# DeltaNet stage: the output gate's projection moved from the inverse into the chain, the loop over heads written out, the convolution of v split over two levels

## The chip, the core and the metric

One core of one Trainium2 chip runs the whole program. The metric is device microseconds of one execution, median of the runs. TensorE does the matmuls, VectorE (DVE in the rows), ScalarE (ACT) and GpSimd (POOL) the element-wise work, SyncE (SP) issues the DMAs here. A matmul takes a stationary operand, which is loaded first (LDWEIGHTS, PEld in the rows), and a moving one, and writes PSUM, which has 8 banks of 512 float32 a partition. Every float32 matmul of the program stands as two instructions in the trace.

## What is computed

One layer of a diffusion backbone on 128 context and 512 latent tokens of width 1024. Its token mixer has two branches, a bidirectional gated DeltaNet and a state-space one; the change is in the DeltaNet branch alone. Of each of its 8 heads (width 128; h here is the input of the mixer):

```python
qkv = silu(dwconv_centred(h @ w_qkv, conv_w, conv_b))     # 5 taps over time
q, k = l2norm(q) * DK ** -0.5, l2norm(k)
beta, g = sigmoid(beta_raw), -exp(a_log) * softplus(a_raw + dt_bias)
# for each direction, chunk by chunk: T = (I + strict(beta k k^T * decay))^-1
v_new = T @ (v * beta) - T @ (k * beta * exp(gc)) @ S
o = (q * exp(gc)) @ S + (q k^T * decay) @ v_new
S = S * exp(g_last) + kdec^T @ v_new
# the sum of both directions
o = rms(o_fwd + o_bwd) * norm_w * silu(h @ w_z)            # the output gate
```

`h @ w_z` is the projection that the change moves. The final states S of both directions are outputs too.

## The kernel before

`build` runs stages one after the other; `deltanet` is one of them, between 690 and 1531 us of the profiled execution. Each engine has its program, written as a Python function, and the engines are ordered by semaphores alone: what stands where in an engine's queue is laid out by hand.

The 640 tokens are 5 tiles of 128 (tile 0 is the context). Each head h goes through `inverse(h)` and `chain(h)`. Constants n = h + 1, K, Q, V, Z = 0 to 3.

**Projections.** `proj(n, j, i)` (L665) is a fifth of projection j of head n: i = 0 to 3 are two of the 8 blocks of the inner dimension each, over the 512 latent tokens (L672), i = 4 all 8 blocks over the 128 context tokens (L675). Latent results go to bank 5 (K, V) or 6 (Q, Z), context results to bank 7. ScalarE copies K, Q, V out (`raw`, L909, L910), VectorE convolves them over time (`convolve`: one tensor-scalar at L1124, then four scalar-tensor-tensor taps at L1126, each waiting for the one before), ScalarE takes tanh (`tanh`, L916), VectorE makes the silu of it (`silu`, L1135, L1136). The squares of k and q (L920) are summed over columns by TensorE (`sums`, L695), kept by VectorE (`keep_sums`, L1141), and GpSimd takes the inverse root (`roots`, L1054). TensorE turns k (`turn_k`), VectorE scales it to kn (`keep_kn`, L1153), TensorE turns kn back (`turn_kn`), ScalarE keeps it (`keep_knT`, L929, L930). v is turned by `turn_v` and kept in `vt` by `keep_v` (L934, L935). The turns are L681.

**Inverse.** The triangular inverse of 10 blocks (5 tiles, two directions) in three groups is built in 6 levels: TensorE multiplies (`blocks_DT`, L743), turns (`turn_D`, L752) and multiplies (`blocks_X`, L735); ScalarE copies the results out (L954, L959) and VectorE masks X (`mask_X`, L1185, and for the last group L1190 adds the identity). At five places i of each level l, `between` puts other work in TensorE's queue: the rest of K's projection of the next head in level 0, Q's in level 1, V's in level 2, **the gate's projection of the current head in level 3** (for head 0 it stands in the prologue), the sums in level 4, the turns of kn and v in level 5. VectorE and ScalarE do the matching steps between their own: `convolve` in levels 1 to 3, `silu` in 2 to 4, `keep_sums`, `gate` and `keep_kn` in level 4. The gate is tanh on ScalarE (`tanh_z`, L924, L925, into `zth`, which shares the memory of R, vn, vd, qs) and `gate` on VectorE (L1145, L1146, into `zg`); `gated` (L1208, L1209) multiplies the turned output of the previous head by it in level 0. Before the levels stand the first two fifths of K's projection, then L809 and turns that start the inverse.

**Chain.** Five steps p; step 0 is the context tile, steps 1 to 4 take one tile forward and one backward. In each TensorE multiplies the state by k and q (KS L848, QS L851; not in step 0), VectorE forms R (L1247 in step 0, else L1249), TensorE VNEW = T R (L855), ScalarE scales it twice (vd L1012, vn L1017), TensorE makes the state's update SU from vd (L867; not in step 4), VectorE the state (L1257, L1259), TensorE the output product O from vn (L875), VectorE adds it to `osum` (L1273, L1276), GpSimd adds the scaled QS (L1078, L1080). Between them stands work for the next head: the k-k and k-q products (L719), the decay sums (`segments`, L726, L727), ScalarE's exponentials (`decay`, L941, L943) and copies (L949), VectorE's masks (`strict`, L1160; `keep_M`, L1168; L1174, L1179 in step 4). GpSimd builds the masks of the next head (L1060, L1064) when level 5 has its last X.

**Loops and loads.** Heads 0 and 7 are written out; heads 1 to 6 are a loop of the engine itself with two heads in its body (`Fori(1, GH - 2, 2)`, three rounds) on TensorE, ScalarE, GpSimd and VectorE, and a loop over one head on SyncE, for heads 1 to 5. SyncE's `body(h)` waits for the last QS of the head before and loads a state, waits for head h+1's three projections and loads K, Q, V weights of head h+2, waits for the gate's projection (`g_z`) and loads the next gate weights, then stores the context's final states. Before the loop the prologue of TensorE is: all four projections of head 0, sums, turns, products, segments.

The order in the prologue and the chain's heart before:

```python
for j in range(4):                       # prologue, L886
    for i in range(5): ...; proj(0, j, i)
sums(0, 0); turn_kn(0, 0); turn_v(0, 0)
for b in range(3): products(0, 0, b)
segments(0)
inverse(0, 0, first=True); chain(0, 0)
```

## Time and profile before

| | us |
|---|---|
| median of 3 runs | 2403.32 (2402.17 to 2407.29) |
| the profiled execution | 2399.45 |
| its span, first to last instruction | 2397.6 |
| TensorE busy in the span | 2137.0 (89%) |
| VectorE busy | 999.7 (42%) |
| ScalarE busy | 540.0 (23%) |
| GpSimd busy | 274.5 (11%) |
| mean granted TensorE clock, 1 is 2.4 GHz | 0.950 |

In the rows below a line of a view in order of time has the start in us from the span's start, the length in us, the engine, the line of the kernel, the operation, output and inputs, shapes and how many instructions were merged, and in brackets the time for which the engine stood idle before it and what ended that: an engine with the line of its instruction, or "issue", when nothing in the profile released it. Lengths of matmuls overlap with the start of the next: what an instruction takes of TensorE's time is read from start to start. In the view by windows the columns are the window, its length, and for PE, PEld, DVE, ACT and POOL the busy us with the number of instructions, then the granted clock, the DMA share and GB/s. In the view by line: the group, its count, busy us and mean ns, and idle us before it.

### The profile page before, as it was taken

To read this page: it belongs to the slowest core of one execution; us is meant where nothing else is said; L and a number is where in the kernel's file an instruction comes from. 1 tells how busy PE (TensorE), PEld (TensorE's weight loads), DVE (VectorE), ACT (ScalarE), POOL (GpSimd) and SP (SyncE) were. 2 spreads that over 40 slices of the span, in tenths; PEclk is the share of its full clock that TensorE was granted. 3 is DMA by queue.
4 is the path that set the end of the run, shared out by engine and by line. 5 is a ranking of instruction groups with operands and counts; after the bars stand their busy time and mean duration, and the time that the engine had idled before them with its cause. 6 is when DMAs were issued, how large, how long until landed. Compare 5 with 4: busy or idle time off the path is not lost. (4 is left out here: it accounts for less than half of the span.)

```text
span 2397.6 us, 26673 instructions
## 1 busy us (share of the span) xinstructions
PE 2137.0 (89%) x10098; PEld 1329.9 (55%) x10098; DVE 999.7 (42%) x1920; ACT 540.0 (23%) x1283; POOL 274.5 (11%) x325
## 2 busy tenths in 40 slices
PE   3899999999978998989989898799999795799985
PEld 1555555555545777767767777455555444443332
DVE  3446556555544555544545544200000066322224
ACT  1323213233112433333333334200000000011111
POOL 0020020201110102111110211100000000321112
PEclk9899999999988999999999999999999896799998
DMA  8121201211020100101011001495322365499983
GB/s 292 51 62 44 53 10 44 62 44 36 9 66 12 38 25 18 36 6 38 4 40 30 11 11 30 145 297 174 110 79 80 125 247 202 139 396 413 398 324 136
DMA packets 177806, 260.06 MB, mean 108 GB/s; under 512 B 14759, under 2 KB 146664, under 8 KB 163344
## 3 DMA queue, kind: packets, MB, share of 16 engines
q1 hardware_dynamic: 151096, 219.04, 26.6%
q10 hardware_dynamic: 18488, 23.54, 3.4%
q0 software_dynamic: 8096, 15.75, 1.8%
q8 instruction: 84, 1.38, 0.2%
q14 instruction: 42, 0.34, 0.0%
HBM read 231.78 MB, written 39.10 MB: 113 GB/s over the span
## 5 line engine op out<-in xcount | busy, mean ns | idle before, releaser
L672 PE MATMUL bank<-hT,shared 128*128 128x512 f32 x512 | 244.9, 608 | 14.0 <-DMA shared<-in_w_in_dram 7.9
L1421 PE MATMUL bank<-hT,shared 128*128 128x512 f32 x384 | 169.3, 594 | 2.6 <-DVE xT L1794 1.8
L2393 PE MATMUL bank<-ring,xgT 128*64 128x512 f32 (+1 forms) x416 | 150.1, 627 | 13.7 <-DMA ring<-in_w_exp_up_dram 9.9
L1185 DVE TENSOR_TENSOR X<-bank,negm 128x512 f32<-128x512 f32 x144 | 81.8, 599 | 185.7 <-PE bank L735 185.5
L1476 PE MATMUL bank<-wz,hT 128*128 128x512 f32 x320 | 152.5, 614 | 0.0
L672 PEld LDWEIGHTS bank<-hT,shared 128*128 128x128 f32 x512 | 91.5, 196 | 89.2 <-issue 81.1
L743 PE MATMUL bank<-DT,X 128*128 128x128 f32 x960 | 128.8, 277 | 2.4 <-DVE X L1185 2.4
L743 PEld LDWEIGHTS bank<-DT,X 128*128 128x128 f32 x960 | 119.9, 192 | 17.0 <-issue 13.4
L735 PE MATMUL bank<-D_,MT 128*128 128x128 f32 x960 | 125.2, 280 | 0.0
L1975 DVE SCALAR_TENSOR_TENSOR prod<-gth,bank 128x512 f32<-128x512 f32 x16 | 11.0, 687 | 272.1 <-PE bank L1945 272.1
L954 ACT COPY D_<-bank 128x512 f32<-128x512 f32 x144 | 73.3, 515 | 215.8 <-PE bank L752 215.6
L1421 PEld LDWEIGHTS bank<-hT,shared 128*128 128x128 f32 x384 | 71.1, 190 | 84.3 <-issue 84.1
L735 PEld LDWEIGHTS bank<-D_,MT 128*128 128x128 f32 x960 | 117.2, 196 | 0.4
L1945 PE MATMUL bank<-yT,wm 128*128 128x512 f32 x256 | 111.2, 592 | 0.0
L2393 PEld LDWEIGHTS bank<-ring,xgT 128*64 128x64 f32 (+1 forms) x416 | 56.5, 165 | 96.5 <-issue 96.5
L1945 PE MATMUL bank<-hT,wm 128*128 128x512 f32 x224 | 98.0, 595 | 0.0
L959 ACT COPY DT<-bank 128x512 f32<-128x512 f32 x144 | 74.0, 518 | 95.5 <-PE bank L743 94.4
L1476 PEld LDWEIGHTS bank<-wz,hT 128*128 128x128 f32 x320 | 59.5, 196 | 63.2 <-issue 63.2
L1465 PEld LDWEIGHTS bank<-xT,M 128*128 128x128 f32 x640 | 78.6, 197 | 19.3 <-DVE xT L1776 11.1
L752 PEld LDWEIGHTS bank<-cst,DT 128*128 128x128 f32 x480 | 61.3, 146 | 46.6 <-issue 46.3
L1744 DVE SCALAR_TENSOR_TENSOR sroom<-spadded,scw,sroom 128x644 f32<-128x644 f32 x96 | 85.4, 890 | 3.4
L1126 DVE SCALAR_TENSOR_TENSOR conv<-padded,cw,conv 128x644 f32<-128x644 f32 x96 | 85.4, 890 | 3.4
(405 smaller groups left out, 3394.6 us busy)
## 6 DMA issues: line engine op xcount, KB each, us to landing
shared<-in_w_in_dram SPq DMA_DIRECT2D x62, 512.0 KB, 5.5
ring<-in_w_exp_gate_dram SPq DMA_DIRECT2D x26, 1024.0 KB, 12.9
ring<-in_w_exp_up_dram SPq DMA_DIRECT2D x26, 1024.0 KB, 17.6
ring<-in_w_exp_down_dram SPq DMA_DIRECT2D x26, 1024.0 KB, 14.6
aw<-in_w_ada_dram SPq DMA_DIRECT2D x8, 2048.0 KB, 9.6
yd<-mzero ACTq DMA_DIRECT2D x1, 16128.0 KB, 107.2
aw<-in_w_ada_dram SPq DMA_DIRECT2D x8, 1024.0 KB, 21.1
wz<-in_w_in_dram SPq DMA_DIRECT2D x4, 2048.0 KB, 7.9
```

The source lines that it names most:

```text
L672: pe.matmul(bank[LATB[j]][:, :], wof(j)[:, k, :], hT[:, k, SEQ:T], start=(k == 0), stop=(k == KD - 1), skip_group_check=True)
L735: last = pe.matmul(xdv(g)[:, u * P:(u + 1) * P], MT[:, u0 + u, :], D_[:, u0 + u, :], start=True, stop=True, skip_group_check=True)
L743: last = pe.matmul(dtv(g)[:, u * P:(u + 1) * P], X[:, u0 + u, :], DT[:, u0 + u, :], start=(g == 2), stop=(g == 2 or l == LEVELS - 1), skip ...
L959: act.copy(DT[:, u0:u0 + m, :], tiles4(dtv(g))).then_inc(s["g_DTkept"], 1)
L1126: ins = STT(out=to, in0=x[:, k:k + CW], scalar=cw[:, k, j:j + 1], in1=to, op0=ALU.mult, op1=ALU.add)
L1185: ins = TT(out=X[:, u0:u0 + m, :], in0=tiles4(xdv(g)), in1=mask, op=ALU.mult)
L1421: pe.matmul(bank[a][:, :], wn(n)[:, k, :], hT[:, k, SEQ:T], start=(k == 0), stop=(k == KD - 1))
L1465: last = pe.matmul(bank[Y][:, h * SP_:(h + 1) * SP_], M[:, u % 2, h, :], dtx[:, d, h * SP_:(h + 1) * SP_], start=(d == 0 and h == 0), stop ...
L1476: last = pe.matmul(bank[Z][:, :], hT[:, k, t * P:(t + 1) * P], wz[:, k, :], start=(k == 0), stop=(k == KD - 1), skip_group_check=True)
L1744: ins = STT(out=c3, in0=padded[:, n % 3, k:k + CW], scalar=cw[:, k, n:n + 1], in1=c3, op0=ALU.mult, op1=ALU.add)
L1945: last = pe.matmul(bank[j][:, :], W(at + k), src[:, k, SEQ:T], start=(k == 0), stop=(k == kk - 1))
L2393: last = pe.matmul(bank[2 + slot][at, :], xgT[:, slot, k, at], wgu[w][:, k, :, :], start=(k == 0), stop=(k == KD - 1))
```

## The change

The gate's projection of head h leaves level 3 (and the prologue) for `chain(h)`: its latent part is written in eight chunks of one block each (`gate_lat`), one after QS and one after VNEW in steps 1 to 4, into bank 0; its context part (`gate_ctx`) in chunks of two blocks after O in steps 1 to 3 and one after VNEW in step 4, into bank 2. `tanh_z` and `gate` stand at the end of the chain on ScalarE and VectorE, `zth` is a part of `th`, and the next inverse waits for the gate before it writes banks 0 and 2. The loops over heads are Python loops, on all engines. v's projection starts one place later (latent part in level 2, context part in level 3); its first two taps are in level 3, its last three in level 4, its tanh and silu in step 0 of the chain; its turn and copy stand in levels 1 and 2 of its own head's inverse, with one buffer in place of two. In the prologue the segments, the decay and the strict masks come ahead of the sums.

```diff
-        vt = S("vt", [P, 2, NT, P])
+        vt = S("vt", [P, NT, P])
-        zth = small4[:, :, :, :].rearrange("p a d n -> p (a d n)")[:, 0:T]
+        zth = th[:, 0:T]
-        LATB = (5, 6, 5, 6)
+        LATB = (5, 6, 5, 0)
+        CTXB = (7, 7, 7, 2)
@@ sync
-                with sp.Fori(1, GH - 2) as h:
+                for h in range(1, GH - 2):
                     body(h)
@@ tensor
+                def gate_lat(h, k):
+                    pe.matmul(bank[LATB[Z]][:, :], wof(Z)[:, k, :], hT[:, k, SEQ:T], start=(k == 0), stop=(k == KD - 1), skip_group_check=True)
+
+                def gate_ctx(h, ks):
+                    for k in ks:
+                        last = pe.matmul(bank[CTXB[Z]][:, 0:P], wof(Z)[:, k, :], hT[:, k, 0:SEQ], start=(k == 0), stop=(k == KD - 1), skip_group_check=True)
+                    return last
-                def turn_v(n, h):
-                    pe.wait_ge(s["g_zg"], h + 1)
-                    pe.wait_ge(s["g_silu"], 3 * n + 3)
-                    pe.wait_ge(s["g_knT"], n + 1)
-                    turned(vT, 6, P, s["g_vturn"])
+                def turn_v(h, more):
+                    if more:
+                        pe.wait_ge(s["g_raw"], 3 * h + 4)
+                    pe.wait_ge(s["g_silu"], 3 * h + 3)
+                    turned(vT, 5, P, s["g_vturn"])
@@ between
-                    if l == 2 and more:
-                        if i == 0 or i == 4:
-                            pe.wait_ge(s["g_raw"], 3 * n + 1 + i // 4)
-                        proj(n, V, i)
-                    if l == 3:
-                        if more and i == 4:
-                            turn_k(n)
-                        if not first:
...
-                            proj(h, Z, i)
+                        if i == 4:
+                            turn_v(h, more)
+                    if l == 2 and more and i > 0:
+                        if i == 1:
+                            pe.wait_ge(s["g_v"], h + 1)
+                        proj(n, V, i - 1)
+                    if l == 3 and more and i == 0:
+                        pe.wait_ge(s["g_raw"], 3 * n + 2)
+                        proj(n, V, 4)
+                    if l == 3 and more and i == 4:
+                        turn_k(n)
-                    if l == 5 and more and i == 2:
-                        turn_v(n, h)
@@ inverse, before the first product
+                    if not first:
+                        pe.wait_ge(s["g_zg"], h)
@@ chain, step p, after QS
+                            if p == 1:
+                                pe.wait_ge(gw[Z], 16 * h + 16)
+                                if more:
+                                    pe.wait_ge(s["g_dec"], n + 1)
+                                else:
+                                    pe.wait_ge(s["g_DTkept"], 18 * h + 18)
+                            gate_lat(h, 2 * p - 2)
@@ after VNEW
+                        if p > 0:
+                            gate_lat(h, 2 * p - 1)
+                        if p == 4:
+                            gate_ctx(h, range(6, 8)).then_inc(s["g_z"], 1)
@@ after O
+                        if 1 <= p <= 3:
+                            gate_ctx(h, range(2 * p - 2, 2 * p))
@@ prologue
-                for j in range(4):
+                for j in (K, Q, V):
...
-                sums(0, 0)
+                pe.wait_ge(s["g_gm"], 1)
+                segments(0)
+                turn_k(0)
+                sums(0)
                 turn_kn(0, 0)
-                turn_v(0, 0)
                 for b in range(3):
                     products(0, 0, b)
-                segments(0)
                 inverse(0, 0, first=True)
                 chain(0, 0)
-                with pe.Fori(1, GH - 2, 2) as h:
-                    for a in range(2):
-                        inverse(h + a, 1 - a)
-                        chain(h + a, 1 - a)
+                for h in range(1, GH - 1):
+                    inverse(h, h % 2)
+                    chain(h, h % 2)
@@ scalar, inverse
+                        if l == 2:
+                            keep_v(h)
-                        if more and 1 <= l <= 3:
+                        if more and 1 <= l <= 2:
                             raw(n, l - 1)
-                        if l == 4 and not first:
-                            tanh_z(h)
-                        if more and 2 <= l <= 4:
-                            tanh(n, l - 2)
+                        if more and 2 <= l <= 3:
+                            tanh(n, l - 2, wait=(l == 3 or not first))
                         keep_DT(h, l, 0)
+                        if more and l == 3:
+                            raw(n, V)
@@ scalar, chain, end of step 0 and end of the chain
                             decay(h + 1)
+                            tanh(h + 1, V)
...
+                    tanh_z(h)
@@ vector, inverse
-                        if more and 2 <= l <= 4:
+                        if more and 2 <= l <= 3:
                             silu(n, 1 - par, l - 2)
-                        if more and 1 <= l <= 3:
+                        if more and 1 <= l <= 2:
                             convolve(n, l - 1)
-                        if l == 4:
-                            if more:
-                                keep_sums(n)
-                            if not first:
-                                gate(h)
-                            if more:
-                                keep_kn(n, 1 - par)
+                        if more and l == 3:
+                            convolve(n, V, taps=range(2))
+                        if more and l == 4:
+                            keep_sums(n)
+                            convolve(n, V, taps=range(2, TAPS))
+                            keep_kn(n, 1 - par)
@@ vector, chain, after the output sum of step 0 and at the end
+                        if more and p == 0:
+                            silu(n, 1 - par, V)
...
+                    gate(h)
```

The loops of ScalarE, GpSimd and VectorE are written out in the same way as TensorE's.

## Rows read from the trace of the kernel before

**Rows 1.** Busy time by head: microseconds, busy per engine (count), granted clock, DMA share, GB/s.
```profile
848.02:947.24 99.22, 92.27 (x580) 71.48 (x579) 52.85 (x115) 36.25 (x95) 14.10 (x20) 1.00 0.10 25
947.24:1051.84 104.60, 94.60 (x579) 72.34 (x578) 52.87 (x115) 36.25 (x95) 14.11 (x20) 0.97 0.09 24
```

**Rows 2.** TensorE in order of time, last head's levels 2 to 4: start, length, instructions.
```profile
1474.56 1.95 PE L743 MATMUL bank<-DT,X 128*128 128x128 f32 x16
...
1480.22 1.06 PE L743 MATMUL bank<-DT,X 128*128 128x128 f32 x8
...
1492.65 1.95 PE L675 MATMUL bank<-hT,shared 128*128 128x128 f32 x16
1494.44 1.95 PE L743 MATMUL bank<-DT,X 128*128 128x128 f32 x16
```

**Rows 3.** TensorE in order of time, start of head 4's inverse, level 5 and chain.
```profile
1148.45 3.60 PE L672 MATMUL bank<-hT,shared 128*128 128x512 f32 x8
1151.89 1.02 PE L809 MATMUL bank<-DT,cst 128*128 128x512 f32 x2
...
1219.85 1.16 PE L743 MATMUL bank<-DT,X 128*128 128x128 f32 x8 [0.42 <-DVE X L1185]
...
1231.90 0.71 PE L855 MATMUL bank<-small,DT 128*128 128x128 f32 x4 [0.26 <-DVE small L1249]
...
1237.12 0.71 PE L855 MATMUL bank<-small,DT 128*128 128x128 f32 x4 [1.23 <-DVE small L1249]
...
1240.51 0.61 PE L851 MATMUL bank<-state,kq 128*128 128x128 f32 x4
1241.41 0.71 PE L855 MATMUL bank<-small,DT 128*128 128x128 f32 x4 [0.29 <-DVE small L1249]
1242.84 0.71 PE L867 MATMUL bank<-small,shared 128*128 128x128 f32 x4 [0.71 <-ACT small L1012]
...
1244.25 0.71 PE L848 MATMUL bank<-state,kq 128*128 128x128 f32 x4 [0.18 <-DVE state L1259]
...
1247.12 0.71 PE L875 MATMUL bank<-small,att 128*128 128x128 f32 x4 [0.71 <-ACT small L1017]
```

**Rows 4.** All engines in order of time, from head 2's last step to head 3.
```profile
1041.04 0.71 PE L855 MATMUL bank<-small,DT 128*128 128x128 f32 x4 [0.29 <-DVE small L1249]
...
1044.50 0.47 DVE L1276 TENSOR_TENSOR gboth<-gboth,bank 128x128 f32<-128x128 f32 x2
...
1046.23 5.78 PE L672 MATMUL bank<-hT,shared 128*128 128x512 f32 x8 [3.05 <-issue]
```

**Rows 5.** VectorE in order of time, prologue.
```profile
724.30 0.69 DVE L1136 SCALAR_TENSOR_TENSOR kq<-th,conv 128x512 f32<-128x512 f32 x1
```

**Rows 6.** Groups of instructions of the DeltaNet stage by line.
```profile
L1126 DVE SCALAR_TENSOR_TENSOR conv<-padded,cw,conv 128x644 f32<-128x644 f32 x72 | 64.1, 890 | 2.5
...
L916 ACT ACTIVATE th<-conv 128x644 f32<-128x644 f32 x18 | 13.5, 750 | 0.0
...
L1160 DVE TENSOR_TENSOR D_<-dec,D_ 128x640 f32<-128x640 f32 x12 | 9.8, 819 | 0.0
```

**Rows 7.** ScalarE in order of time, first step of head 4's chain.
```profile
1229.70 1.08 ACT L943 ACTIVATE dec<-bank 128x512 f32<-128x512 f32 x2
```

**Rows 8.** TensorE in order of time, prologue.
```profile
729.72 2.39 PE L695 MATMUL bank<-cst,gboth 128*128 128x1 f32 x20 [1.48 <-ACT gboth L920]
...
745.53 3.60 PE L672 MATMUL bank<-hT,shared 128*128 128x512 f32 x8
753.07 1.64 PE L809 MATMUL bank<-DT,cst 128*128 128x512 f32 x2 [3.94 <-DVE DT L1179]
```

**Rows 9.** VectorE in order of time, head 4, level 4.
```profile
1215.58 0.17 DVE L1141 TENSOR_SCALAR ssum<-bank 128x10 f32<-128x10 f32 x1 [1.59 <-PE bank L695]
```

**Rows 10.** GpSimd in order of time, head 4, level 4.
```profile
1215.83 1.95 POOL L1054 TENSOR_TENSOR rn<-ssum,half 128x10 f32<-128x10 f32 x1 [54.42 <-DVE ssum L1141]
```

**Rows 11.** Line 1190 (X plus identity): shortest, median, longest in ns.
```profile
L1190 DVE TENSOR_TENSOR X<-X,cst x48: 424/426/1508, 760.7 to 1500.9; 128x256 f32<-128x256 f32 x48
```

More of the change, by code:

```diff
@@ L1039, in _ @@
                 chain(0, 0)
-                with act.Fori(1, GH - 2, 2) as h:
-                    for a in range(2):
-                        inverse(h + a, 1 - a)
-                        chain(h + a, 1 - a)
+                for h in range(1, GH - 1):
+                    inverse(h, h % 2)
+                    chain(h, h % 2)
                 inverse(GH - 1, 1, more=False)
@@ L1096, in _ @@
                 chain(0, 0)
-                with pool.Fori(1, GH - 2, 2) as h:
-                    for a in range(2):
-                        chain(h + a, 1 - a)
+                for h in range(1, GH - 1):
+                    chain(h, h % 2)
                 chain(GH - 1, 1, more=False)
```

104 lines of the change are left out of this document (44 added, 60 removed).

## The prediction

> **What bounds the kernel now.** I read the busy time by head first. In the DeltaNet stage TensorE is busy in 92.27 of the 99.22 us of an ordinary head [rows 1], and VectorE, ScalarE and GpSimd in half of it or less. So a head lasts as long as TensorE's program: six levels of the inverse, then the chain of five steps. The second view is TensorE's own order in time. In the last head, where the inverse has nothing beside it but the gate projection, a bare level runs from 1474.56 to 1480.22, 5.66 us, with no wait. The level that holds the gate projection runs to 1494.44, 14.22 us [rows 2]. So the inverse has no idle time for the projection to fill: it costs 14.22 - 5.66 = 8.56 us a head. Third, the chain [rows 3], where TensorE waits in every step: 0.3 us (once 1.23) for VectorE's R, 0.7 for ScalarE's scaled copies, 0.2 for the state. That idle time is what the change fills. Fourth, heads 2 and 4, at whose ends the loop returns to its top, last 104.60 us instead of 99.22 [rows 1]; the surplus shows as 3.05 us marked "issue" and eight matmuls in 5.6 us instead of 3.44, right behind the last product of the chain [rows 3, 4].
>
> **The sum**, against the profiled execution: 2399.45 us, 3.87 under the median of 2403.32; its span is 2397.6.
>
> 1. Gate projection out of level 3, heads 1 to 7: 7 x 8.56 = **-59.9**. V's context part (the same form, 8 matmuls of 128 columns, 1.79 us by 1492.65 to 1494.44 [rows 2]) only goes from level 2 to level 3, and the turn of v from level 5 to level 1: nothing. The cover of a level without filler is shown by the last head: 5.66 with no wait. With q's silu, ScalarE's copy of V and two taps beside it, TensorE's 8 us for level 3 still exceed the DVE's some 5.4.
>
> 2. The loops written out. The return to the loop's top happens twice (after heads 2 and 4): 2 x (104.60 - 99.22) = **-10.8**. About 3.1 of the 5.4 is TensorE waiting for nothing but its next instruction, the rest the eight matmuls after it, partly at 1.2 instead of 2.4 GHz (granted clock 0.97 over the head against 1.00 [rows 1]). The Trainium skill's Runtime: NRT & Kernel Launch, section Instruction fetch mechanics, says that a taken branch out of the fetched window stalls while code in a straight line streams unseen; the boundary row agrees, the sum stands without it. Bounds: 0 and 10.8.
>
> 3. Prologue, where today head 0's gate projection runs before anything of the chain: q's silu ends at 724.99 on VectorE [rows 5], and a square of 0.74 (as ScalarE's tanh, 0.750 [rows 6]) follows, so the column sums could start at 725.9; they start at 729.72 since ScalarE sits in the gate's tanh first: -3.8. From products to inverse, the segment products, ScalarE's decay (0.4 + 1.08 [rows 7]) and two strict masks of 0.82 [rows 6] move ahead of the sums, 2.0 + 1.5 + 1.6, into idle time: -5.1 of the 7.5 us between 745.53 and 753.07 and the 2 before it [rows 8]. Together **-9**, bounds -4 (only the sums come earlier) and -12 (the low clock there goes too).
>
> 4. The chain pays. One pass of a gate chunk over 512 columns is 3.44 / 4 = 0.86 us (1148.45 to 1151.89 [rows 3]), two context chunks 0.45.
> - Chunk between QS and the product after it (step 3): QS starts at 1240.51, the product at 1241.41, 0.90; QS fills 0.45 of it. A chunk makes 1.31: +0.41. In step 2 the product waits 1.23 for VectorE anyway: 0.
> - Chunk after that product: next product 1.43 later (1241.41 to 1242.84), 0.45 + 0.86 = 1.31 fits: 0.
> - Two context chunks after the output product: 1242.84 to 1244.25 is 1.41 and holds two groups of products of 0.54 and 0.45; with 0.45 more it is 1.44: +0.03.
> - Last step: a chunk and two context chunks, 0.45 + 0.86 + 0.45 = 1.76 against 1.43 (0.71 idle at 1247.12 [rows 3]): +0.33.
> - Step 1 has V's silu (0.29 + 0.68 with overlap, 0.9) ahead of R on VectorE. ScalarE's decay ends at 1230.78 [rows 7]; tanh 0.75 behind it, silu 0.9, R 0.6: R would be ready at 1233.1, and the product that takes it starts at 1231.90 today [rows 3]: +1.2, and 0.1 for the wait's end: +1.3. (The turn of v no longer stands ahead, which takes 0.55 from both alike and is paid in level 1.)
> Sum for heads 0 to 6: 1.3 + 0 + 0.44 + 0.44 + 0.33 = 2.5, **+17.5**. Last head, no silu and no masks: 4 x 0.44 + 0.33 = **+2.1**. Bounds a head: 1.2 (silu hidden) and 5 (each chunk exposed by half more).
>
> 5. Level 4: VectorE now has three taps between the sums it keeps and the writes of kn. A tap is 0.89 with 0.03 between [rows 6]. Sums are kept at 1215.58 + 0.17 [rows 9], GpSimd's root ends at 1215.83 + 1.95 = 1217.78 [rows 10]; three taps end at 1218.5. kn, and behind it the mask X that level 5 waits for already (0.42 at 1219.85 [rows 3]), come 0.7 later. 7 x 0.7 = **+4.9**, bounds 0 and 1.5 a head. Split in two the taps otherwise cost nothing: all five in the short level 3 would pass its mask by 2.
>
> 6. Handover. Bank 0 and bank 2 hold the gate, so the next inverse waits for VectorE's gate(h), which is queued behind first blocks, add one and the last output sum: that sum ends at 1044.97, 3.9 us after the last product that R feeds (1041.04 [rows 4]); it starts 0.4 earlier against that product now, and the gate adds 0.28 + 0.68, the size of a silu: 4.5. TensorE arrives after 1.76 + 0.45 + 3.44 = 5.65, K's first half covering it: 0. Before head 7 there is no K: 4.5 against 2.2, **+2.3** once.
>
> 7. DMAs. SP's load of the next gate weights, the state store and, behind them, the next state's load are queued behind the gate's end in the chain rather than in level 3; the weights are wanted a whole inverse (some 60 us) later: 0. Q, K, V loads wait one level longer, also with tens of us in hand. GpSimd gets no work. ScalarE's tanh of the gate stands before the next keep D, both after TensorE's K half: 0.
>
> Total -59.9 - 10.8 - 9 + 17.5 + 2.1 + 4.9 + 2.3 = **-52.9**: 2346.5 in a profiled execution of that kind, and 3.87 more, **2350**, as median.
>
> **Rivals.**
> - *Boundary stays.* The 5.4 us belong to code fetch that long straight code pays too. For it: the code grows threefold. Against it: heads 0, 1 and 7 stand in or enter straight code without it. +10.8: 2361. Chance 0.08.
> - *VectorE and GpSimd block each other in level 4.* The taps read two tensors in SBUF while GpSimd takes its root. The row for X plus identity shows such a pairing: 424 ns alone, 1508 beside GpSimd's masks [rows 11]. If the taps wait for the whole root, 1.95 a head: +13.7, 2364. Against it: most of the 1.95 on 10 columns is not reading, and if GpSimd waits for a tap instead, its result is wanted only after the third. Chance 0.06. The Trainium skill's SBUF — State Buffer, section Who interferes with whom, states this as a rule against the change: a VectorE instruction with two SBUF inputs and a GpSimd one that reads SBUF exclude each other for a whole instruction. By it the sum would be 2364; no row here shows a tap beside a root.
> - *The gate isn't covered* (the other side). If products of the chain are issued no earlier than now after each chunk, all 8.67 us of a projection land in the chain, 7.5 more a head than counted: 8 x 7.5 = +60, 2410. It takes 52.9 / 8 = 6.6 us a head to turn the sign. Against it: the 0.7 us waits are on ScalarE, which doesn't wait for gate chunks, and banks 0 and 2 are free. Chance 0.03; half of it, 0.02, gives 2380.
> - *More comes back*: silu finds VectorE idle, the prologue gives 12, no wait in level 5: -3 - 9 - 4.9 against the sum, partly: 2338. Chance 0.11.
>
> **The numbers.** The forecast has 0.70: 2350, own range 2340 to 2360. The range 2338 to 2366 takes in the first two rivals and most of the last; outside it stays under 0.2. About 0.2% (5 us) is what a measurement can tell from no change: faster 0.95, same 0.02, slower 0.03.
>
> **What will show it.** Level 3 near 8 us for heads 1 to 6, 5.7 for head 7, with no L672 matmuls in it but V's. Chain steps: 4.7 us where they were 4.3, 5.2 kept in step 2, about 7 from the first to the second. No 3 us "issue" gap in the stage. A wait near 1.1 for X at level 5. Inverse of head 0 starting near 744. Heads of some 93 to 94 us. Wrong if the 0.7 us waits for vd stay beside the chunks, if level 3 shows waits of over 0.5, or if straight code shows gaps marked "issue".

## The result and the profile after

The changed kernel takes **2336.72 us** (median of 4 runs, 2334.37 to 2337.98), the kernel before 2402.74 in the 4 runs beside it: ratio 0.9727, 95% interval 0.9715 to 0.974, 66 us less. The forecast was 2350.0 with a range of 2338 to 2366: the direction and the mechanism held, the time lies 1.3 us below the range. Profiled execution against profiled execution it is 2399.45 to 2336.3, -63.15, where the sum said -52.9. The other 2.9 us are the distance of profile and median: 3.3 in the runs of before beside it, 0.4 in those of after.

The head of the page after, then, in a second fence, busy time by head with the columns of [rows 1]:

```profile
span 2334.2 us, 25709 instructions
...
PE 2110.1 (90%) x10098; PEld 1314.7 (56%) x10098; DVE 995.9 (43%) x1920; ACT 540.4 (23%) x1283; POOL 276.2 (12%) x325
```

```profile
835.70:928.86 93.16, 90.30 (x580) 70.38 (x579) 52.08 (x115) 36.27 (x95) 14.68 (x20) 1.00 0.10 26
928.86:1022.00 93.14, 90.28 (x579) 70.39 (x578) 51.65 (x115) 36.28 (x95) 16.38 (x20) 1.00 0.10 26
```

These are heads 1 and 2. A head has as many TensorE instructions as before and lasts 93.2 us instead of 99.22 or 104.60 [rows 1], with 2.9 us of it idle instead of 6.95. Next, TensorE in order of time for head 4's levels 3 to 5, its chain and the start of head 5, the stretch that answers to [rows 3]:

```profile
1159.05 1.05 PE L751 MATMUL bank<-DT,X 128*128 128x128 f32 x8
1159.94 1.95 PE L676 MATMUL bank<-hT,shared 128*128 128x128 f32 x16
...
1167.06 1.95 PE L751 MATMUL bank<-DT,X 128*128 128x128 f32 x16
...
1176.02 1.16 PE L751 MATMUL bank<-DT,X 128*128 128x128 f32 x8 [1.00 <-DVE X L1201]
...
1181.78 0.61 PE L866 MATMUL bank<-small,DT 128*128 128x128 f32 x4
...
1188.51 0.71 PE L866 MATMUL bank<-small,DT 128*128 128x128 f32 x4 [0.48 <-DVE small L1264]
1189.05 1.02 PE L680 MATMUL bank<-hT,shared 128*128 128x512 f32 x2
1189.93 0.71 PE L882 MATMUL bank<-small,shared 128*128 128x128 f32 x4
...
1193.73 0.71 PE L866 MATMUL bank<-small,DT 128*128 128x128 f32 x4 [0.37 <-DVE small L1264]
...
1198.42 0.61 PE L866 MATMUL bank<-small,DT 128*128 128x128 f32 x4
...
1203.01 0.61 PE L866 MATMUL bank<-small,DT 128*128 128x128 f32 x4
...
1205.21 3.60 PE L673 MATMUL bank<-hT,shared 128*128 128x512 f32 x8
1208.64 1.02 PE L814 MATMUL bank<-DT,cst 128*128 128x512 f32 x2
```

Level 3 lasts 1167.06 - 1159.05 = 8.01 us and holds no projection but V's context part (L676). In the chain a gate chunk (L680) stands where the wait of 0.7 us for ScalarE was, and the product behind it (L882) waits for nothing. From product to product (L866) the four steps take 6.73 (1181.78 to 1188.51), 5.22, 4.69 and 4.59. Before, they were 5.72 (from the first line below to the L855 at 1231.90 in [rows 3]), 5.22, 4.28 and 4.28:

```profile
1226.18 0.61 PE L855 MATMUL bank<-small,DT 128*128 128x128 f32 x4
...
1245.69 0.71 PE L855 MATMUL bank<-small,DT 128*128 128x128 f32 x4 [0.28 <-DVE small L1249]
```

The output products go straight over into K's projection, with no "issue" gap [rows 4].

The prologue, on TensorE in order of time [rows 8]:

```profile
723.10 4.24 PE L703 MATMUL bank<-cst,gboth 128*128 128x1 f32 x20 [4.06 <-ACT gboth L935]
731.59 1.33 PE L690 MATMUL bank<-cst,shared 128*128 128x128 f32 x5 [4.26 <-DVE shared L1169]
733.76 4.00 PE L727 MATMUL bank<-kq 128*128 128x256 f32 x10 [0.84 <-ACT kq L946]
...
742.62 1.10 PE L814 MATMUL bank<-DT,cst 128*128 128x512 f32 x2 [1.43 <-DVE DT L1195]
```

From the stage's first projection to the first product of the inverse it takes 54.97 us instead of 62.83. The sums start 4.0 us earlier against that first projection, but take 4.24 instead of 2.39 at a low clock. The wait ahead of the inverse is 1.43 instead of 3.94.

**Where the time went, head by head.** Each row is the distance from one head's first product of the inverse (L809 before, L814 after) to the next head's; head 7 counts to the first instruction of its last product T R.

| | before | after | measured | forecast |
|---|---|---|---|---|
| prologue | 62.83 | 54.97 | -7.9 | -9 |
| head 0 | 94.95 | 93.06 | -1.9 | +3.2 |
| head 1 | 99.21 | 93.16 | -6.1 | -5.4 |
| head 2 (returned) | 104.60 | 93.16 | -11.4 | -10.8 |
| head 3 | 100.05 | 93.48 | -6.6 | -5.4 |
| head 4 (returned) | 104.68 | 93.16 | -11.5 | -10.8 |
| head 5 | 101.10 | 93.16 | -7.9 | -5.4 |
| head 6 | 96.97 | 92.27 | -4.7 | -3.1 |
| head 7 | 65.14 | 60.27 | -4.9 | -6.5 |
| sum | | | -62.9 | -53 |

### The profile page after: what moved, and what is told of

Same layout as the page of the kernel before. It is cut to its first block and busy times, and to the rows that moved or that the text cites. A ratio compares the mean times of both kernels' runs of the same rounds, so it can differ in the third digit from the quotient of the medians.

```text
span 2334.2 us, 25709 instructions
## 1 busy us (share of the span) xinstructions
PE 2110.1 (90%) x10098; PEld 1314.7 (56%) x10098; DVE 995.9 (43%) x1920; ACT 540.4 (23%) x1283; POOL 276.2 (12%) x325
## 5 line engine op out<-in xcount | busy, mean ns | idle before, releaser
L673 PE MATMUL bank<-hT,shared 128*128 128x512 f32 x384 | 180.6, 600 | 8.0 <-DMA shared<-in_w_in_dram 8.0
L1433 PE MATMUL bank<-hT,shared 128*128 128x512 f32 x384 | 169.3, 594 | 2.6 <-DVE xT L1806 1.8
L1433 PEld LDWEIGHTS bank<-hT,shared 128*128 128x128 f32 x384 | 71.1, 190 | 84.3 <-issue 84.1
L673 PEld LDWEIGHTS bank<-hT,shared 128*128 128x128 f32 x384 | 67.9, 193 | 63.3 <-issue 55.1
L2141 PE MATMUL bank<-ring,shared 128*128 128x512 f32 x160 | 72.9, 617 | 15.4 <-DMA ring<-in_w_o_dram 15.4
```

Of the source, the lines that this page charges most:

```text
L673: pe.matmul(bank[LATB[j]][:, :], wof(j)[:, k, :], hT[:, k, SEQ:T], start=(k == 0), stop=(k == KD - 1), skip_group_check=True)
L1433: pe.matmul(bank[a][:, :], wn(n)[:, k, :], hT[:, k, SEQ:T], start=(k == 0), stop=(k == KD - 1))
```

## The experiments

The table leaves 10 us to explain. The theory for them: the terms of the sum are right in kind, but it priced every head as head 1, and left standing what heads 0, 3, 5 and 6 had beside it. Rivals: the written-out loops bring more than the 5.4 us a return (other engines' loops too), or the gate costs the chain less than counted.

**1. The loops written out alone.** Kernel before, with all loops over heads written out:

```diff
-                with pe.Fori(1, GH - 2, 2) as h:
-                    for a in range(2):
-                        inverse(h + a, 1 - a)
-                        chain(h + a, 1 - a)
+                for h in range(1, GH - 1):
+                    inverse(h, h % 2)
+                    chain(h, h % 2)
```

> The kernel before with the loops over heads written out on every engine and nothing else. Theory (the two returns of the loop cost 5.4 us each): 10.8 us less than before, ratio 0.9955, heads 2 and 4 at 99.2 us, no gap marked issue. Rival (code fetch is paid in straight code too): within 3 us of before, with new gaps marked issue in heads 1 to 6. Rival on the clock (the return to the top also brings the low clock of other heads): 14 to 17 us less, and the stretches at 1.2 GHz in heads 3, 5 and 6 gone.

2392.57 us, ratio 0.9946 (0.993 to 0.9963). The DeltaNet stage is 10.5 us shorter, against 10.8 of the sum. The end of head 2 on TensorE:

```profile
1049.72 0.71 PE L875 MATMUL bank<-small,att 128*128 128x128 f32 x4 [0.72 <-ACT small L1016]
1050.26 3.60 PE L672 MATMUL bank<-hT,shared 128*128 128x512 f32 x8
1053.70 1.02 PE L809 MATMUL bank<-DT,cst 128*128 128x512 f32 x2
```

No gap, and 3.44 us for the eight matmuls. But heads 1 to 6 are not all 99.2: they take 100.13, 100.04, 100.91, 99.14, 99.14 and 96.46 (head 6 without K's half). So head 4 is at the 99.2 that was expected, but head 2 is not: some surplus has moved from heads 5 and 6 to heads 1, 2 and 3, which experiment 3 takes up.

**2. The loops put back, one group at a time**, into the changed kernel: TensorE's, and then those of all the others.

```diff
@@ tensor; in the second kernel scalar, gpsimd, vector and sync instead
-                for h in range(1, GH - 1):
-                    inverse(h, h % 2)
-                    chain(h, h % 2)
+                with pe.Fori(1, GH - 2, 2) as h:
+                    for a in range(2):
+                        inverse(h + a, 1 - a)
+                        chain(h + a, 1 - a)
```

> The changed kernel with TensorE's loop over heads restored, those of the other engines written out. Theory (TensorE's own return is what costs): 10 to 11 us more than the changed kernel, ratio near 0.977, heads 2 and 4 about 5.4 us longer, a gap of 3 us marked issue at each. Rival (the gap is another engine's return, seen from TensorE): the time of the changed kernel, ratio 0.973.

> The changed kernel with the loops of ScalarE, VectorE, GpSimd and SyncE restored, TensorE's written out. Theory: the returns of these engines now stand behind the gate's tanh and product at the end of the chain, whose result TensorE waits for with 1.1 us in hand; a return of 2 to 3 us (VectorE's first work after its return in the kernel before is not needed for 5 us) makes heads 2 and 4 up to 2 us longer: 0 to 4 us more than the changed kernel, ratio 0.973 to 0.975. Rival: all engines' returns cost alike, 10 us more, ratio 0.977.

TensorE's loop: 2347.5, ratio 0.9766 (0.9745 to 0.9787). The others': 2339.93, 0.9733 (0.9717 to 0.9749), DeltaNet stage 767.09 us to the last of the four instructions of its last product T R, where the changed kernel has 767.03. The two returns of TensorE, in order of time:

```profile
1024.74 0.61 PE L890 MATMUL bank<-small,att 128*128 128x128 f32 x4
1028.11 3.70 PE L673 MATMUL bank<-hT,shared 128*128 128x512 f32 x8 [2.77 <-issue]
1031.64 1.02 PE L814 MATMUL bank<-DT,cst 128*128 128x512 f32 x2
...
1217.93 5.39 PE L673 MATMUL bank<-hT,shared 128*128 128x512 f32 x8 [2.84 <-issue]
1223.16 1.02 PE L814 MATMUL bank<-DT,cst 128*128 128x512 f32 x2
```

The return of TensorE's queue lengthens head 2 by 3.0 us, and head 4 by 4.8, where the matmuls behind it run at the low clock (5.39 us for eight): 7.8 together, under the 10 to 11 that were expected. The whole time of the two kernels, run side by side, is 7.6 us apart. Returns of the other four queues cost nothing that the stage shows. The Trainium skill's Runtime: NRT & Kernel Launch, section Instruction fetch mechanics, has a taken branch out of the fetched window stall and straight code stream on unseen. The traces agree: 2.8 us idle at each return of TensorE, and no such gap behind heads 2 and 4 where its program is written out. The prediction's rival that the boundary's cost stays in straight code is out.

**3. The kernel before once more**, with no edit.

> The kernel before, unchanged, for a second trace. If the stretches at 1.2 GHz in heads 0, 3, 5 and 6 follow from what the program does, they stand at the same places and the head lengths are the same within 0.3 us (94.95, 99.21, 104.60, 100.05, 104.68, 101.10, 96.97). If they fall by chance, the two heads with the returns keep theirs and the others move by 1 to 2 us. Ratio 1.000.

2404.37 us, heads 0 to 6 94.94, 99.21, 104.67, 100.0, 104.65, 101.09 and 97.48. Six of them agree within 0.1 us, head 6 is 0.5 longer: at its end three VectorE instructions (L1174) take 1.88 us beside 1.46 for two of GpSimd (L1080), where the first execution has 1.62 beside 3.15. Here are windows of 3.4 us, with the columns of [rows 1], of the kernel before in the first execution:

```profile
1320.10:1323.50 3.40, 3.40 (x18) 3.40 (x18) 1.96 (x7) 1.54 (x3) 1.95 (x1) 0.50 0.00 0
1323.50:1326.90 3.40, 3.40 (x33) 3.40 (x32) 2.65 (x6) 0.65 (x3) 1.12 (x1) 1.00 0.02 5
```

in the second (its stage starts 1.5 us later):

```profile
1321.60:1325.00 3.40, 3.40 (x18) 3.40 (x18) 2.02 (x8) 1.55 (x3) 1.96 (x1) 0.51 0.00 0
```

and of the kernel with the loops written out alone, where this stretch is gone and others, like one in head 2's inverse, have come:

```profile
1018.40:1021.80 3.40, 3.40 (x18) 3.37 (x17) 1.98 (x6) 1.26 (x4) 1.15 (x1) 0.51 0.00 0
...
1320.10:1323.50 3.40, 2.98 (x27) 2.79 (x26) 3.37 (x8) 0.85 (x2) 2.12 (x2) 1.00 0.00 0
```

The heads' surplus over 99.2 are single stretches of 3.4 us in which the granted clock is 0.50, 1.2 GHz, and TensorE does some half of its matmuls (18, against 33 in the window behind). In heads 0 to 6 they are no accident of one execution: both executions have the same seven there, apart from the returns. In head 7 they can be: the second execution has one 12 us into its inverse, behind the wait of 2.8 us for the turned output, and the first has none; that inverse takes 49.78 us with it and 48.14 without, 1.6 more. They are no property of a head either, since with another length of the heads the seven stand in others. But from head 0's level 1 to head 6 they have only two places, in this kernel and in all the others of this study (a loop's return aside): right behind the sums of level 4, twenty matmuls of one column (some 10 to 12 us ahead of the chain's first product), and in the chain, behind steps with waits (12 to 14 us after that product, 8 to 9 in experiment 5). The kernel before has one at its start in head 0 (after the wait of 3.94 us), behind the sums in heads 0, 5 and 6, and in the chain in heads 0, 3 and 5. The changed kernel:

```profile
1078.30:1081.70 3.40, 3.40 (x18) 3.40 (x17) 3.33 (x8) 1.42 (x3) 2.17 (x1) 0.50 0.00 0
1358.20:1361.60 3.40, 3.40 (x18) 3.40 (x18) 3.33 (x8) 1.37 (x4) 2.07 (x1) 0.50 0.00 0
1406.00:1409.40 3.40, 3.40 (x19) 3.40 (x18) 1.34 (x3) 0.96 (x2) 0.00 (x0) 0.50 0.00 0
```

The wait ahead of the third of them, on TensorE in order of time:

```profile
1404.84 0.77 PE L690 MATMUL bank<-cst,gboth 128*128 128x128 f32 x5 [2.80 <-DVE gboth L1219]
```

The changed kernel has them behind the sums (heads 0, 3 and 6), where they cost 0.3 us instead of 0.9 to 1.1, since level 5 waits 1.00 us behind them anyway, and one in head 7 behind a wait of 2.8 us. This one costs 1.6 us: the inverse of head 7 takes 41.77 us with it, and 40.13 and 40.14 in the kernel of experiment 8 and the second of experiment 4, which have none there. **In the chain the changed kernel has none.** That holds for all ten profiles of kernels of this study with every chunk in the chain (a loop's return aside), in 70 chains ahead of a next head. The kernels with the old waits in the chain have three in seven (the kernel before, both executions, and with its loops out) or six in seven (experiment 5); with one chunk of eight kept there is one, with four kept none (experiment 4). So some 7.4 us of such stretches, of which some 2.7 stood in the chain, became 2.6. With the chunks in the waits, no chain has a stretch; experiment 5, which differs from the changed kernel in the place of the gate's work alone, has them in six chains. But that the empty waits alone bring them is not shown: experiment 4 with one chunk has nearly the waits of the kernel before in steps 2 to 4, and one stretch where that has three. Why one head has a stretch and its neighbour none stays open.

**4. What the gate's chunks cost in the chain.** Only the first of the eight latent chunks kept; then those after QS left out (outputs lack the missing part of the gate):

```diff
@@ gate_lat
-                    pe.matmul(bank[LATB[Z]][:, :], ...)
+                    if k == 0:
+                        pe.matmul(bank[LATB[Z]][:, :], ...)
```

> The changed kernel with one of the eight chunks of the gate's latent projection left in the chain and seven left out, so the output lacks seven eighths of that projection. It asks what the chunks cost where they are now. Theory (they fill waits): step 3 and 4 from 4.69 and 4.59 back to 4.3, the first two steps unchanged at 6.7 and 5.2, 1.0 to 1.3 us a head and 1.6 in the last, 9 to 10 us in all if the clock stays. Clock theory (the chunks in the waits are what keeps the chain at 2.4 GHz): the stretches at 1.2 GHz come back in the chain of three or four heads at 0.8 to 1 us each, so that only 5 to 7 us are left, ratio 0.970 to 0.971. Rival (chunks are exposed in full): 7 x 0.86 us a head, 48 us, ratio 0.953.

> The changed kernel without the chunks between QS and VNEW (half of the gate's latent projection left out), those behind VNEW kept. Theory: those were exposed only in steps 3 and 4 (and 1 to 4 of the last head), 0.4 and 0.3 us: 0.7 x 7 + 1.4 = 6 us less than the changed kernel, ratio 0.970; steps 6.7, 5.2, 4.3, 4.3, and no wait longer than today's behind VNEW. Rival (the chunk behind VNEW delays the next product too): the same 6 us and steps that stay above 4.5.

One chunk: 2334.97, ratio 0.9705 (0.9681 to 0.973). Heads take 92.22 instead of 93.16. The theory that the chunks keep the clock up expected stretches in three or four chains; there is one, in head 0. TensorE in order of time, steps 1 to 3 of head 4's chain:

```profile
1189.12 0.71 PE L867 MATMUL bank<-small,DT 128*128 128x128 f32 x4 [0.48 <-DVE small L1265]
1190.55 0.71 PE L883 MATMUL bank<-small,shared 128*128 128x128 f32 x4 [0.72 <-ACT small L1029]
...
1194.35 0.71 PE L867 MATMUL bank<-small,DT 128*128 128x128 f32 x4 [1.22 <-DVE small L1265]
...
1198.63 0.71 PE L867 MATMUL bank<-small,DT 128*128 128x128 f32 x4 [0.28 <-DVE small L1265]
```

Without the chunks the waits of [rows 3] are back (0.72, 1.22, 0.28), and the last two steps are 4.28 again. So seven chunks of 0.86 us, 6.0 us of TensorE's time, cost 0.94 us a head, which the sum had at 0.41 + 0.41 + 0.33 = 1.15. The stage is 4.5 us shorter than in the changed kernel, less than these 0.94 a head, as head 0 has the stretch in its chain and head 7 one more at its start. In the whole time neither this kernel nor the next can be told from the changed one. Without the four after QS alone: 2333.74, 0.971 (0.9687 to 0.9732); steps 3 and 4 are 4.28 again, the end of the chain (from its last product T R to the next head's first) 5.74, where it is 5.41 with one chunk, and heads 92.60. So the chunk after QS is what steps 3 and 4 pay, and the chunk in the last step adds the 0.33 of the sum.

**5. The gate back in level 3**, of all eight heads (head 0's too, which no longer has it in the prologue), its tanh and product in level 4, everything else as changed:

```diff
-        LATB = (5, 6, 5, 0)
-        CTXB = (7, 7, 7, 2)
+        LATB = (5, 6, 5, 6)
+        CTXB = (7, 7, 7, 7)
@@ between, level 3
+                        if i < 4:
+                            gate_lat(h, 2 * i)
+                            gate_lat(h, 2 * i + 1)
+                        else:
+                            gate_ctx(h, range(8)).then_inc(s["g_z"], 1)
```

> The changed kernel with the gate's projection back in level 3 (of every head), its tanh and product in level 4, all else as changed. Theory: 8 x 8.56 in the inverse, less the 0.94 a head that the chain pays for it, 1.6 in the last head and 2.2 at head 7's start, plus 0.9 a head since the gate's product stands ahead of the taps in level 4: 63 to 66 us more than the changed kernel, level with the kernel before, ratio 0.998 to 1.000. Rival (a bare level 3 hides less, so the projection filled real waits there): 50 us or less, ratio under 0.994, with waits in the changed kernel's level 3 that vanish here.

2406.44 us, ratio 1.0013 (1.0002 to 1.0023): all of the gain is gone, though the loops are written out. TensorE, head 3, level 5 and the chain:

```profile
1119.58 1.16 PE L751 MATMUL bank<-DT,X 128*128 128x128 f32 x8 [1.71 <-DVE X L1204]
...
1132.08 0.71 PE L873 MATMUL bank<-small,DT 128*128 128x128 f32 x4 [1.34 <-DVE small L1270]
1133.51 1.22 PE L885 MATMUL bank<-small,shared 128*128 128x128 f32 x4 [0.72 <-ACT small L1031]
```

An inverse is 75.57 - 66.30 = 9.27 us longer: 8.56 for the projection, as read from [rows 2], and 0.71 more wait in level 5, as the gate's product is again among VectorE's work of level 4. The chain gives back 0.94, but with its waits (1.34, 0.72) there is low clock there too: 1.22 us for four matmuls that take 0.71 at 2.4 GHz. Eight heads of 8.3 are 67 us; the stage is 68.9 us longer than in the changed kernel, with 1.7 less at the handover to head 7 and more stretches of low clock (13 in the stage instead of 7, its ends included). The whole time is 67.1 us longer than that of the changed kernel beside it (experiment 9), where 63 to 66 were expected.

**6. v's taps and v's silu.** All five taps in level 3; v's silu in step 1 behind R instead of in step 0 ahead of it; and that with the third tap in level 3:

```diff
@@ vector, level 3 and 4: taps in one level; the third kernel has range(3) and range(3, TAPS)
-                            convolve(n, V, taps=range(2))
+                            convolve(n, V)
...
-                            convolve(n, V, taps=range(2, TAPS))
@@ vector, chain, step p: silu moved
                         last.then_inc(s["g_R"], 1)
+                        if more and p == 1:
+                            silu(n, 1 - par, V)
...
-                        if more and p == 0:
-                            silu(n, 1 - par, V)
```

> The changed kernel with all five taps of v's convolution in level 3, none in level 4. Theory: in the bare level 3 VectorE is through with them at 8.1 us, when level 4 should have its X: a wait of 0.9 us for X there, as head 0 had one of 0.69 in the kernel before; the wait of 1.0 us at level 5 falls to 0.4. In all +0.3 a head, 2 us more than the changed kernel, ratio 0.9735. Rival (the split is what makes the bare level possible): 2 us a head or more, 14 us, ratio 0.979. Rival (the split costs): 3 us or more less than the changed kernel.

> The changed kernel with v's silu moved from the end of step 0, where R of step 1 waits behind it, to right behind R of step 1, where VectorE waits for SU for 2.2 us. Theory: step 1 falls from 6.73 to between 5.7 and 6.1 (the gate's chunk then fills its wait), the others stay: 0.6 to 1.0 us in heads 0 to 6, 5 to 7 us less than the changed kernel, ratio 0.970. Rival (ScalarE's tanh ahead of the scaling of QS is what delays step 1, or the decay's end that the gate's chunk waits for): no change.

> The changed kernel with v's silu behind R of step 1 and three of v's taps in level 3, two in level 4. Theory: steps 6.1 and 5.1 as measured with the silu alone (5.4 us in all), and the wait for X at level 5 from 1.0 to between 0.1 and 0.4 with none new at level 4, 0.6 a head: 9 to 10 us less than the changed kernel, ratio 0.968 to 0.969. Rival (GpSimd's root is delayed by the taps, so that kn isn't earlier): the 5.4 us of the silu alone, ratio 0.9705.

Taps in one level: 2342.82, ratio 0.9744 (0.9723 to 0.9766). A head without a low stretch is only 0.16 us longer than with the taps split (a wait of 0.47 at level 4, and 0.43 instead of 1.00 at level 5); most of the rest of the stage's 5 us are stretches. Split or not makes next to nothing of the change. Silu moved: 2330.23, 0.969 (0.9667 to 0.9714). TensorE in step 1 of head 4:

```profile
1188.04 0.61 PE L866 MATMUL bank<-small,DT 128*128 128x128 f32 x4
```

It has no wait (0.48 above), the first step takes 6.09 instead of 6.73, and a head 92.41 instead of 93.16. The third tap, expected to give 4 us more, gave nothing: 2328.4, 0.9687 (0.9666 to 0.9708), the same heads, and still a wait of 0.99 at level 5. In the changed kernel this is VectorE in level 4 of head 4:

```profile
1171.26 2.73 DVE L1142 SCALAR_TENSOR_TENSOR conv<-padded,cw,conv 128x644 f32<-128x644 f32 x3
1173.98 1.39 DVE L1169 TENSOR_SCALAR shared<-bank,rn 128x128 f32<-128x128 f32 x5
```

and GpSimd beside it:

```profile
1171.42 2.53 POOL L1069 TENSOR_TENSOR rn<-ssum,half 128x10 f32<-128x10 f32 x1 [46.41 <-DVE ssum L1157]
```

The root takes 2.53 us, where it took 1.95 without taps beside it [rows 10]. Its end, 1173.95, and that of the three taps, 1173.99, coincide. So one tap less only shows the other limit, VectorE in level 4 with two taps:

```profile
1175.56 1.38 DVE L1169 TENSOR_SCALAR shared<-bank,rn 128x128 f32<-128x128 f32 x5 [0.92 <-POOL rn L1069]
```

The root takes 2.53 us there as well, and kn waits for GpSimd. What holds it up is not the number of taps beside it, but the one that already runs when it starts. In experiment 5 the gate's product stands ahead of the taps, and they start 0.63 us after the root, GpSimd and then VectorE in head 3:

```profile
1114.27 1.96 POOL L1072 TENSOR_TENSOR rn<-ssum,half 128x10 f32<-128x10 f32 x1 [54.96 <-DVE ssum L1160]
```

```profile
1114.90 2.73 DVE L1145 SCALAR_TENSOR_TENSOR conv<-padded,cw,conv 128x644 f32<-128x644 f32 x3
```

There the root takes 1.96 us though taps run beside it, and the three taps take their 2.73 as well. The gate's product, which runs at the root's start there and in the kernel before and reads one of its inputs from PSUM, costs the root nothing. With all taps in level 3 (first kernel of this experiment) it is 1.96, too. In the changed kernel the first tap runs 0.72 us on after the root's start, and the root loses 0.58.

**7. The taps out of level 4 altogether**: v's last three taps in step 0 behind R, and the silu in step 1; beside it the kernel with the silu moved alone, again.

```diff
@@ vector, inverse, level 4
-                            convolve(n, V, taps=range(2, TAPS))
@@ vector, chain, behind R
+                        if more and p == 0:
+                            convolve(n, V, taps=range(2, TAPS))
```

> The changed kernel with v's silu in step 1 of the chain (as in the run before it) and v's last three taps in step 0 right behind R, where VectorE stands idle for 5.19 us in that run; level 4 keeps only the sums and kn. If GpSimd's root is held up by the taps beside it, it takes 1.95 us again instead of 2.53, kn comes 0.6 us earlier, and the wait for X at level 5 falls from 1.0 to about 0.4 us: heads near 91.8 us against 92.41, the DeltaNet stage near 757.5 against 761.6, ratio to the kernel before near 0.967. If the wait at level 5 is set by VectorE's own queue of masks, heads stay at 92.4 and the ratio at 0.969. If the taps in step 0 delay the first state, the step from the first to the second product grows from 6.09 and the heads with it.

> The kernel with v's silu in step 1 alone once more, beside the run above on the same chip: heads 92.4 us, ratio 0.969.

GpSimd and, in a second fence, TensorE at the start of level 5, in head 3:

```profile
1078.67 1.96 POOL L1069 TENSOR_TENSOR rn<-ssum,half 128x10 f32<-128x10 f32 x1 [46.41 <-DVE ssum L1157]
```

```profile
1082.70 1.16 PE L751 MATMUL bank<-DT,X 128*128 128x128 f32 x8 [0.42 <-DVE X L1201]
```

The root is back at 1.96 and the wait at level 5 at the 0.42 of [rows 3], and heads take 91.85 against 92.42: 0.57 less. The stage is 759.97 against 761.68 us, where 757.5 was expected; two of its heads (92.75, 92.73) have a low stretch that costs 0.9, as little is left of the wait behind it. In all it is 2331.35, ratio 0.9706 (0.9688 to 0.9724), against 2328.84, 0.9692 (0.9676 to 0.9709): no difference in the whole time that these runs can tell.

**8. The prologue's order put back**: segments, decay and strict masks behind the sums again, the gate still out of it.

```diff
@@ tensor; the decay on scalar and the strict masks on vector go behind as well
-                pe.wait_ge(s["g_gm"], 1)
-                segments(0)
                 turn_k(0)
...
                 for b in range(3):
                     products(0, 0, b)
+                segments(0)
```

> The changed kernel with the old order in the prologue: segments, decay and strict masks behind the products, not ahead of the sums. Theory: the inverse of head 0 starts 5 us later (742.6 to 747.7), ratio 0.975. Rival (the sums' and the turns' chain sets it in either order): under 2 us, ratio 0.973 to 0.9735.

2341.56, ratio 0.9738 (0.9717 to 0.9759). TensorE in the prologue:

```profile
724.96 4.43 PE L703 MATMUL bank<-cst,gboth 128*128 128x1 f32 x20 [5.16 <-ACT gboth L934]
...
748.99 1.97 PE L814 MATMUL bank<-DT,cst 128*128 128x512 f32 x2 [3.94 <-DVE DT L1194]
```

The wait of 3.94 us ahead of the inverse is back, and behind it the low clock: 1.97 us for two matmuls of 512 columns, where 1.02 is usual. The prologue is 4.3 us longer than in the changed kernel beside it (experiment 9; 5.1 in the sum), head 0 another 1.7. In the whole time the two can't be told apart.

**9. The changed kernel again**, beside experiments 5 and 8.

> The changed kernel, unchanged, on the chip of these runs, as what they are held against. Ratio 0.9727. If its low-clock stretches follow from what the program does they stand in heads 0, 3, 6 and 7 again, and the heads' lengths are the same within 0.1 us.

2339.33, ratio 0.9731 (0.9714 to 0.9747). Six of the heads 0 to 6 agree with the first profile within 0.1 us as expected, head 6 is 0.4 longer, and the stretches of low clock stand at the same places in each head, head 7 included.

**The fastest kernel** is the changed one with v's silu in step 1 (with or without the other taps moved): 2328.4 to 2331.35 in the four runs of three kernels, some 0.4% under the changed kernel. The stage is 5.3 to 7.1 us shorter in their traces. In the whole time one of them ran beside the changed kernel, that with the third tap moved, and there the intervals are just apart (0.9666 to 0.9708 against 0.9714 to 0.9747); of the other three intervals, from other sets of runs, one overlaps with that of the changed kernel and one touches it.

## Why the forecast was right in kind and 13 us too high

Right, with what was measured for it:

- *Gate out of level 3* (-8.56 a head, with +0.7 in level 4: -7.86): the inverse is 7.99 shorter in heads 1, 2 and 4, level 3 is 8.01, the wait at level 5 is 1.00 (1.1 forecast). Experiment 5 shows the same price from the other side.
- *Loops* (-10.8): 10.5 by experiment 1, in the kernel before; put back into the changed one TensorE's loop costs 7.8, as one of its two returns has no low clock behind it (experiment 2). It is TensorE's loop alone.
- *Prologue* (-9): -7.9. The order gives 4.3 to 4.5 of it by experiment 8 (5.1 forecast). The other 3.4 come with the old order too, from the absence of the gate and of v's turn (3.8 forecast, for the gate): the sums start 4.0 us earlier, but at the low clock they take 1.9 more.
- *Handover to head 7* (+2.3): 4.42 instead of 2.23, +2.2. Both move by 0.4 to 0.5 from one execution to the next (4.82 and 2.75 in the second ones), so the agreement to 0.1 is luck.

The steps that failed:

- **The sum took head 1 as every head.** "7 x 8.56" and "2 x 5.4" price differences against a bare head of 99.22. But heads 3 and 5 of the trace before took 100.05 and 101.10, and head 6's inverse 0.94 more than head 1's, which no term named, and head 0's inverse had 69.2 us where its bare parts, as after shows, are 66.2. What stood in head 0 was 1.7 us of low clock at its start, 1.2 in level 3 (VectorE had all five of V's taps there) and two more stretches. They went: 4.6 us in head 0, net, and 3.0 in heads 3, 5 and 6; head 7 got one of 1.6 instead. The prediction looked at TensorE's clock only at the returns and put all other low clock of the stage at nothing; the same view in windows of a few us would have shown it, part of it in the chain, behind the waits that the change fills. The range should have had a term from 0 to -7 for it.
- **Term 4, +2.5 a head, was too dear**: 1.95 measured. V's silu and the first step's chunk cost 1.01 (1.3), of which 0.64 goes when the silu is moved, the chunk in step 3 exactly its 0.41, in step 4 0.31 (0.44), the end 0.22 (0.33). The context chunks cost nothing. 7 x 0.55 = 3.9 us too much. In the last head the row has +1.5 for +2.1; another 0.31 is paid behind the last product T R, where the row ends.
- **Head 7's inverse** is 6.4 us shorter, not 8.56. The low stretch takes 1.6 of it; without one it is 40.13 us (experiment 8), 8.0 shorter than before. The other 0.55 is the turn of v in level 1, which the sum let cancel although nothing of it left the last head's level 5. The stretch is partly luck: the second execution of the kernel before has one there too.
- **The shift to the median, +3.87**, took a distance of one profiled execution from its median for a constant. In the runs of after it is 0.4. Such a distance belongs in the range, not in the forecast.

Added up against the 9.9 us by which the stage beat the sum: prologue +1.1, chain -3.9 and -0.6, low clock and head 0's waits -7.6, the inverse's 0.13 a head -0.8, head 7's inverse +2.2: -9.6. The range's lower end had the case "more comes back" at 2338, but built from silu, prologue and level 5, of which little came; the clock's share was not in it.

*The rivals.* "VectorE and GpSimd block each other" had the right place and the wrong size. The root is held up by 0.58 us, not the taps by 1.95, and experiment 7 gets the 0.57 back. The Trainium skill's SBUF — State Buffer, section Who interferes with whom, has two such instructions exclude each other. The traces agree in one direction only: the root waits for a tap that runs when it starts (0.16 us after the tap's start in the changed kernel) and loses 0.58, less than the 0.72 that this tap still takes. The other way round no tap waits: those that start while the root runs keep their 0.9 us each, in the changed kernel and in experiment 5, where the root started first. So term 5 (+0.7 a head, 0.57 measured) had a second cause of the same size beside the taps' length, and taking one tap out could not show anything. "The gate isn't covered" is refuted by experiment 4: 0.94 us a head instead of 7.5 more.

## What to carry to other kernels

Work that fills an engine's waits costs what it overhangs there, and the row of the wait tells it beforehand: a chunk of 0.86 us where TensorE waited 0.7 was nearly free, the same chunk where it waited 0.3 cost 0.3 to 0.4. Before a sum is made per iteration, list all iterations with their lengths and give every surplus over the shortest a line; where it is a low clock of TensorE, look whether the waits ahead of it are among those that the change fills. Where an instruction on a second engine is what everybody waits for, less work of the first engine beside it did not help (experiment 6); what counted was that no tap ran when that instruction started, because the taps had been moved away (experiment 7) or stood behind it (experiment 5).

## What was not expected of the hardware

- Stretches of 3.4 us at 1.2 GHz (granted clock 0.50) stand at the same places of heads 0 to 6 in two executions of one kernel, and in other heads when the heads' length changes. In the heads of these kernels they come behind twenty one-column matmuls, behind a loop's return or behind waits. The same stretch costs 0.8 to 1.1 us in dense work, 0.3 ahead of a wait and 1.6 in the last head's inverse.
- TensorE's return to its loop's top left a gap of 2.8 to 3.2 us six times out of six; behind five of them eight matmuls took 5.4 to 5.9 us, behind one 3.7, near the usual 3.6. The returns of four other queues cost nothing.
- A GpSimd power over 10 columns takes 1.95 us without taps beside it, 2.53 when one of VectorE's taps already runs at its start, with two or three taps alike, and 1.96 when the taps start 0.63 us after it.
